# A hybrid encoder layer on one core: the first weight unit in blocks, logits ahead of the last value product, a raw buffer for the last output unit, one GpSimd split at the router's end

## The reference

```python
def token_mixer(x, ...):
    proj = rms_norm(x, norm_g) @ w_in        # dq, dk, dv, nq, nk, nv (512 columns each), gates (2048)
    # differential attention: 4 heads, two softmax maps each, T5 bias
    o = (softmax(q1 k1 + bias) - lam * softmax(q2 k2 + bias)) @ dv
    # lam = exp(sum(lq1*lk1)) - exp(sum(lq2*lk2)) + lambda_init
    y_diff = rms_norm(o, diff_subln) * (1.0 - lambda_init)
    # neighbourhood attention: 8 heads, windows of 8 rows x 16 columns on a grid 64 wide
    y_na = neighborhood_attention(nq, nk, nv, na_rpb)
    merged = g_diff * (y_diff @ w_br_diff) + g_na * (y_na @ w_br_na)
    return x + merged @ w_out

def expert_choice_ffn(h, w_router, w_gate, w_up, w_down):   # h = rms_norm(x, norm2_g)
    aff = softmax(t @ w_router)              # 16 experts
    gate, idx = top_k(aff.T, cap)            # 32 prompt and 64 sample tokens for each expert
    he = silu(xe @ wg) * (xe @ wu)           # EXPERT_FF 2816
    y = zeros.at[idx].add((he @ wd) * gate)
```

## Time and profile before

| | |
|---|---|
| time, median of 3 runs | 2210.21 us (2209.09 to 2210.94) |
| the profiled execution | 2212.8 us, of which its span is 2211.0 us |
| instructions | 27257 |
| mean granted clock of TensorE | 0.987 |
| TensorE busy | 2128.8 us (96%) |
| VectorE busy | 1582.0 us (72%) |
| ScalarE busy | 1370.8 us (62%) |
| GpSimd busy | 238.7 us (11%) |
| chain that ended last | PE 82%, DMA 7%, DVE 6%, ACT 4%, issue 1% |
| data moved | 623.97 MB, mean 282 GB/s |

### The profile page before, as it was taken

One profiled execution on the slowest core, in us unless ns is written; L12 is line 12 of the kernel. 1 busy time (PEld: TensorE's weight loads), 2 busy tenths in 40 slices (PEclk: granted clock), 3 DMA queues, 4 the chain that ended last, 5 costly groups with the idle time before them and its releaser, 6 DMA issues.

```text
span 2211.0 us, 27257 instructions
## 1 busy us (share of the span) xinstructions
PE 2128.8 (96%) x10388; PEld 1592.4 (72%) x10388; DVE 1582.0 (72%) x1249; ACT 1370.8 (62%) x1102; POOL 238.7 (11%) x137
## 2 busy tenths in 40 slices
PE   6999999999968999999999999999999999999997
PEld 5867888887756767777677776767767677777765
DVE  5374363233456888888888888888888888888885
ACT  5364364122225777777777777777777777777764
POOL 2202120000130001010101102011010201101010
PEclk9999999999988999999999999999999999999999
DMA  5111141113436999999999999999999999999995
GB/s 232 58 36 67 58 144 60 64 58 115 162 118 236 373 370 366 376 371 385 364 368 385 367 378 370 373 373 370 378 365 380 365 374 385 367 376 374 375 372 184
DMA packets 71389, 623.97 MB, mean 282 GB/s; under 512 B 8272, under 2 KB 8656, under 8 KB 18608
## 3 DMA queue, kind: packets, MB, share of 16 engines
q1 hardware_dynamic: 63264, 595.62, 69.6%
q0 software_dynamic: 7648, 27.40, 4.4%
q10 hardware_dynamic: 432, 0.34, 0.0%
HBM read 609.70 MB, written 13.63 MB: 282 GB/s over the span
## 4 chain that ended last, share of the span: by engine, by line
PE 82%; DMA 7%; DVE 6%; ACT 4%; issue 1%; POOL 0%; ACTq 0%; SPq 0%; DVEq 0%; POOLq 0%
PE PS L527 25%; PE PS L529 25%; PE PS L528 25%; DMA x_w_raw<-in_w_expert_gate 5%; DVE x_w_low L1160 4%; ACT x_w_high L1090 3%; PE PS L625 2%; PE PS L610 2%; PE PS L872 1%; DMA x_w_raw<-in_w_expert_up 1%; PE PS L638 1%; PE PS L536 1%; PE PS L815 1%; PE PS L736 0%; DMA cst<-in_consts 0%
## 5 line engine op out<-in xcount | busy, mean ns | idle before, releaser
L1160 DVE TENSOR_TENSOR x_w_low<-x_w_raw,x_w_high 128x2048 fp32r<-128x2048 f32 (+1 forms) x382 | 1174.5, 3086 | 241.9 <-ACT x_w_high L1090 239.6
L1090 ACT ACTIVATE x_w_high<-x_w_raw 128x3072 fp32r<-128x3072 f32 (+1 forms) x384 | 980.0, 2558 | 266.2 <-PE PS L529 190.9
L527 PE MATMUL PS<-x_w_high,xT_high 128*96 128x512 f32 (+1 forms) x1536 | 580.5, 378 | 9.7 <-DVE x_w_low L1160 7.6
L529 PE MATMUL PS<-x_w_high,xT_low 128*96 128x512 f32 (+1 forms) x1536 | 575.4, 375 | 0.0
L528 PE MATMUL PS<-x_w_low,xT_high 128*96 128x512 f32 (+1 forms) x1536 | 573.4, 373 | 0.0
L527 PEld LDWEIGHTS PS<-x_w_high,xT_high 128*96 128x96 f32 x1536 | 248.3, 162 | 105.6 <-DVE x_w_low L1160 18.6
L529 PEld LDWEIGHTS PS<-x_w_high,xT_low 128*96 128x96 f32 x1536 | 248.1, 162 | 90.0
L528 PEld LDWEIGHTS PS<-x_w_low,xT_high 128*96 128x96 f32 x1536 | 248.8, 162 | 85.1 <-issue 0.2
L527 PE MATMUL PS<-x_w_high,hidden_high 128*96 128x512 f32 x704 | 281.3, 400 | 0.0
L529 PE MATMUL PS<-x_w_high,hidden_low 128*96 128x512 f32 x704 | 276.7, 393 | 0.0
L528 PE MATMUL PS<-x_w_low,hidden_high 128*96 128x512 f32 x704 | 275.9, 392 | 0.0
(11 more groups left out here) (185 smaller groups left out, 1774.4 us busy)
## 6 DMA issues: line engine op xcount, KB each, us to landing
x_w_raw<-in_w_expert_gate SPq DMA_DIRECT2D x96, 1536.0 KB, 8.4
x_w_raw<-in_w_expert_up SPq DMA_DIRECT2D x96, 1536.0 KB, 8.8
x_w_raw<-in_w_expert_down SPq DMA_DIRECT2D x96, 1536.0 KB, 8.3
x_w_raw<-in_w_expert_gate SPq DMA_DIRECT2D x32, 1024.0 KB, 7.5
x_w_raw<-in_w_expert_up SPq DMA_DIRECT2D x32, 1024.0 KB, 7.4
x_w_raw<-in_w_expert_down SPq DMA_DIRECT2D x32, 1024.0 KB, 7.0
w_raw<-in_w_in SPq DMA_DIRECT2D x20, 1024.0 KB, 4.8
x<-in_x_sample SPq DMA_DIRECT2D x8, 512.0 KB, 13.5
```

The lines of the kernel that those rows point to most:

```text
L527: mm(out, sh, mh, start=first, stop=False)
L529: return mm(out, sl, mh, start=False, stop=last)
L1090: a_(xh[:, w % SPLITS, 0:n], xraw[:, w % RAWS, 0:n], ACT.Copy).then_inc(x_high, 1)
L1160: return v.tensor_tensor(out, src, high.bitcast(F32), ALU.subtract)
```

## The change

1. *Start.* Unit 0 and the first four token blocks are loaded block by block, in turn; the vectors come first on SyncE's queue. ScalarE and VectorE split them block by block, and TensorE works on unit 0 with the block as the outer loop and the six tiles inside. Constants and lambdas move to GpSimd's queue, behind the fourth token block; the bias tables behind the eighth. The clearing of the keys goes to the projection "pn", the lambda steps to the ends of the first two chunks of "pd".
2. *Projection.* In "pd" the transposes come three steps behind instead of two (`LAG`). The last value product of both projections is issued in step 2 of `attend`, behind the logits of items 0 and 1, and its scaling on VectorE in step 1. In "pn" two tiles are normalised behind value tile 0, and none behind the last.
3. *Output.* Unit 27 has a raw buffer of its own, `w_last`, in the place of its low half, and its load doesn't wait for a split. The reload of x is issued two chunks earlier.
4. *Router end.* GpSimd splits unit 0 alone. VectorE takes the low halves of the tokens and of unit 1 before the slot tables; TensorE doesn't wait for the tables before the first expert.

```diff
+LAG = {"pd": 3, "pn": 2}
...
+        w_last = at("w_raw_last", 50112, UNIT).rearrange("p (k n) -> p k n", k=4)
...
             def load_unit(n, src):
+                if n == UNITS - 1:
+                    stage_done(sp, 5)
+                    sp.dma_start(w_last, src.rearrange("p (k c) -> p k c", k=4)).then_inc(S("o", "last_unit_loaded"), 16)
+                    return
+                if n >= 2:
+                    sp.wait_ge(w_split, n - 1)
                 sp.dma_start(wraw[:, n % 2], src.rearrange("p (k c) -> p k c", k=4)).then_inc(w_loaded[n % 2], 16)
 
-            for u in range(2):
-                for i in (2 * u, 2 * u + 1):
-                    sp.dma_start(xT[:, 2 * i:2 * i + 2, :], x_turned[:, 2 * i:2 * i + 2, :]).then_inc(s_xT[i], 16)
-                load_unit(u, src_of("pd", "q", u))
+            sp.dma_start(rows, vectors).then_inc(s_rows, 16)
+            first = src_of("pd", "q", 0).rearrange("p (k c) -> p k c", k=4)
+            for k in range(4):
+                sp.dma_start(xT[:, k, :], x_turned[:, k, :]).then_inc(S("n1", f"xT_loaded{k}"), 16)
+                sp.dma_start(wraw[:, 0, k], first[:, k]).then_inc(S("n1", f"w_loaded{k}"), 16)
+            for i in range(2, 4):
+                sp.dma_start(xT[:, 2 * i:2 * i + 2, :], x_turned[:, 2 * i:2 * i + 2, :]).then_inc(s_xT[i], 16)
+            load_unit(1, src_of("pd", "q", 1))
...
-                if kind == "out0":
+                if kind == "gate_n1":
...
-            sp.wait_ge(w_high, UNITS)
+            sp.wait_ge(w_high, UNITS - 1)
...
+            pool.wait_ge(S("n1", "tev"), 4)
+            pool.dma_start(cst, consts).then_inc(s_cst, 16)
+            pool.dma_start(lamv, lambdas).then_inc(s_lamv, 16)
+            pool.wait_ge(S("n1", "tev"), KD)
             load_diff(0)
             load_diff(1)
-            pool.wait_ge(s_cst, 32)
+            pool.wait_ge(s_cst, 16)
...
-            for w in range(2):
-                n = unit_width(w)
-                pool.wait_ge(x_high, w + 1)
...
+            n = unit_width(0)
+            pool.wait_ge(x_high, 1)
+            nc.gpsimd.tensor_tensor(xl[:, 0, 0:n], xraw[:, 0, 0:n], xh[:, 0, 0:n].bitcast(F32), ALU.subtract
+                                    ).then_inc(x_split, 1)
...
+                if before is None:
+
+                    for k in range(4):
+                        pe.wait_ge(S("n1", "tev"), k + 1)
+                        pe.wait_ge(S("n1", "w_low"), k + 1)
+                        for t in range(NT):
+                            i = split_product(PS[:, t, :], hTh[:, k, t * P:(t + 1) * P], hTl[:, k, t * P:(t + 1) * P],
+                                              wh[:, 0, k], wl[:, 0, k], k == 0, False)
+                            if k == 3:
+                                i.then_inc(w_prod, 1)
+                    pe.wait_ge(s_cst, 16)
...
-                    if before is None or n >= START_EARLY:
+                    if (NT if before is None else START_EARLY) <= n < len(steps) - 1:
                         chunk_product(chunks, c, u, t, hTh, hTl, bank_free)
                     if u == 1 and c < 2:
                         done_at.append(n)
-                    while jt < len(done_at) and n >= done_at[jt] + 2:
+                    while jt < len(done_at) and n >= done_at[jt] + LAG[stage]:
...
                 for step in range(len(L) + 5):
+                    if step == 2:
+                        chunk_product([c for c in CHUNKS if c[0] == stage], 2, 1, NT - 1, hTh, hTl, None)
...
-            pe.wait_ge(S("rt", "tables"), 2)
...
             for k in range(KD):
-                act.wait_ge(s_xT[k // 2], 16)
+                act.wait_ge(*((S("n1", f"xT_loaded{k}"), 16) if k < 4 else (s_xT[k // 2], 16)))
                 a_(hTh[:, k, :], xT[:, k, :], ACT.Copy, scale=g1[:, k:k + 1]).then_inc(S("n1", "high"), 1)
-                if k % 4 == 3:
-                    split_units(k // 4 + 1)
+                if k < 4:
+                    act.wait_ge(S("n1", f"w_loaded{k}"), 16)
+                    a_(wh[:, 0, k], wraw[:, 0, k], ACT.Copy).then_inc(S("n1", "w_high"), 1)
...
+            def keep_values(stage, t):
+                tile = V_ORDER[stage][t]
+                product_done(dve, [c for c in CHUNKS if c[:2] == (stage, "v")][0], t)
+                v.tensor_scalar(vv[:, tile, :], PS[:, t, :], nrs[:, tile:tile + 1], None, ALU.mult
+                                ).then_inc(S(stage, "pused"), 1)
...
+                            if t < NT - 1:
+                                keep_values(stage, t)
+                            for y in {0: (0, 1), 5: ()}.get(t, (t + 1,)) if stage == "pn" else ():
+                                norm_y(y)
                     if c < 2:
                         scale_proj(stage, NT * c + NT - 1)
+                        if stage == "pd":
+                            (lambda_sums, lambda_factor)[c]()
+                        else:
+                            v.memset(kT[c][64 * (1 - c):64 * (2 - c)], 0.0).then_inc(s_kz, 1)
...
+                    if step == 1:
+                        keep_values({"diff": "pd", "na": "pn"}[br], NT - 1)
...
-            dve.wait_ge(S("rt", "slots"), 1)
-            link(table(0, CS, 3, 1, E))
-            v.tensor_scalar(idxs, idxf[0:CS, :], float(SP_), None, ALU.subtract)
-            v.tensor_copy(idxi[:, 2:E + 1], idxf[:, 2:E + 1]).then_inc(S("rt", "tables"), 1)
...
             for q in range(PRE):
                 misc_low("tokens", q, q + 1, q + 1, 6 + q)
-            dve.wait_ge(x_split, RAWS + 2)
+            dve.wait_ge(x_split, RAWS + 1)
+            unit_low(0, 1)
+            dve.wait_ge(S("rt", "slots"), 1)
+            link(table(0, CS, 3, 1, E))
+            v.tensor_scalar(idxs, idxf[0:CS, :], float(SP_), None, ALU.subtract)
+            v.tensor_copy(idxi[:, 2:E + 1], idxf[:, 2:E + 1]).then_inc(S("rt", "tables"), 1)
             unit_low(0, 2)
```

84 lines of the change are left out of this document (42 added, 42 removed).

## The result

The changed kernel took 2197.4 us (median of 4 runs, 2196.1 to 2197.7), the kernel before beside it 2210.6 us (2209.1 to 2211.1): a ratio of 0.9943, 95% interval 0.9929 to 0.9957. That is a gain of 13.2 us where 20.6 were forecast; it moved the way that the prediction said, and ended 0.9 us above the upper end of the range. The profiled execution took 2197.56 us with a span of 2195.8 us, so the span shrank by 15.2 us.

A forecast was written before the change was run, and what follows sets the result against it. TensorE, busy 96% of the span, was taken to bound the kernel. Gains of 8.8, 0.9, 1.4, 4.1 and 5.35 us summed to 20.6, taking the median from 2210.2 to 2189.6 us; range 2184.0 to 2196.5.

The forecast's parts named there:

- What bounds the kernel: Whole kernel: TensorE is busy 96% of the span; the expert loop has no idle time left, so gains come before it.
- Rivals 2 and 4: Expert loop: head start of its loads was needed, 2194, chance 0.10; or its period grows, 2234 at 350 GB/s, chance 0.03.
- Rival 5: Edits don't do what they say, as the same waits end last for another reason: within 0.2%, chance 0.03.
- Start: Before the first matmul: loading and splitting by blocks starts TensorE at 8.4 instead of 17.2 us, 8.8 us gained.
- Rival 1: Kernel start gives 3 to 5 us less, through slow queue filling, stalls between blocks or the identity table; 2193.5, chance 0.15.
- First attention: Where the first attention begins: value product behind logits 0 and 1 gains 0.9 us, bounds 0 and 3.5.
- Rival 3: First attention and router keep the clock up, and the value windows land in time: 5 us more, 2184.5, chance 0.13.
- Second attention: Where the second attention begins: later value product and earlier normalising gain 1.4 us, bounds 0.2 and 2.6.
- 1.85 - 1.6 + 1.2: Second attention: transposes 1.85 us earlier, a new 1.6 us wait for value windows, a 1.2 us bias-table wait gone.
- Output buffer: Output projection: own raw buffer for the last unit removes a 2.7 us wait and 1.4 us of low clock, 4.1 us.
- Router: Router end: a faster comparison gains 3.0 us, low halves of tokens before the tables 1.75 us.
- Clock at the first expert: Start of the expert loop: without the pause the clock may rise earlier, 0 to 2.4 us, taken as 0.6.

## Why the prediction was right or wrong

**What bounds the kernel: right.** The loop kept its length (1533.85 and 1533.1 us), and all but 0.75 us of the gains and losses lie ahead of it. Rivals 2 and 4, which had the loop or its first loads pay for the start, fall: no wait is left at the first experts. Rival 5 falls too.

**Start: 8.8 forecast, 8.44 at the first matmul, 7.4 in the end.** Two things were missed. The rate: from 4 to 8 us the DMA engines moved 236 GB/s with loads of one block, where the kernel before moved 424 in the same time. The summary of that window after, with SyncE's queue (packets, MB, share of the 16 engines), and then that queue before:

```profile
DMA packets 421, 0.94 MB, mean 236 GB/s; under 512 B 47, under 2 KB 47, under 8 KB 421
q1 hardware_dynamic: 421, 0.94, 91.8%
```

```profile
q1 hardware_dynamic: 194, 1.04, 62.4%
```

Part of the gap is that 0.65 of the 1.69 MB came on the other engines' queues before, whose loads are now moved; SyncE's own queue brings hardly less, but in more than twice as many packets, which fill 92% of the engines' time instead of 62%. I had reckoned with 369 to 410 throughout. The first block needs little, so TensorE started only 0.4 us late, but what follows in the queue, unit 2's load last, comes later, and the bias loads (issued at 19.23 us) now share the engines with it. I had given unit 2's split 2.7 us of room through the later transposes; it was used up, and TensorE waited 0.80 us there (0 to 1.01 us in the other kernels with this start). The run with the bias loads moved has q ready at least 2.1 us earlier, which shows that those loads were part of the delay. Against the run with the old start, whose first matmul came at 17.36 us, 1.1 us are lost between the first matmul and the scores: 0.80 are this wait, 0.2 one slow matmul more at the beginning (seven beside six), 0.1 stays open. Rival 1 (3 to 5 us less) named the right mechanism at three times the size.

I had read the Trainium skill (SBUF — State Buffer, the "DVE blocks DMA" trap) as speaking against moving the constants to GpSimd's queue. It names VectorE operations in a 2-port mode, and whether the two-input passes here are of that kind no run shows. The issue at 13.88 us landed 5.4 us later, between VectorE's passes of 1 us, and TensorE waited for nothing there. No run here shows the trap.

**First attention: 0.9 forecast, 0.7 measured by undoing it.** The reading that logits 2 and not the transposes are in the way was right. The trace showed 1.9 us more, which the clock gave; it had been 0.58 and 0.73 in the kernel before from 129 to 139 us, and in the changed kernel it was 1.00 in one execution and 0.66 for 5 us in another, and with windows by rows it was 0.59 and 0.73 again. Rival 3 took this for a gain that the change might bring. It is not the change's: the kernel before with other loads has it too. In the forecast this row stood at nothing, so its 1.9 us are luck of the executions compared.

**Second attention: 1.4 forecast, -4.8 measured.** This is the step that failed. The sum was 1.85 - 1.6 + 1.2. Its first term was even better, 2.44 us (the transposes of s_na came 84.48 us after those of q before, and 82.04 after). The direction of the second was right, its size wrong. TensorE comes 12.52 us earlier than before (312.92 against 300.40, ready) and the windows' first issue 9.44 us earlier (282.69 and 273.25), so TensorE gains 3.1 us on them; I had said 2.85. But I had the last windows landed at 28.6 us after the first issue, worked out from one microsecond of the queue at 0.10 MB near the end. They took 32.4 us. Of these 3.8 us two bias tables are about 2, by the run that held them back. In the kernel before the first of the two was issued 27.0 us after the first windows, when they were nearly through:

```profile
309.65 0.53 POOL L410 DMA_DIRECT2D bias_windows<-in_bias_sample  x1 [12.11 <-DVE small L1283]
```

Now it is issued at 296.96, 23.7 us after them, with 8.7 us to go, and the next at 301.16, with 4.5 to go. The other 1.7 us are not explained by a run; the 28.6 was an estimate, and all that the trace of the kernel before shows is that the windows had landed by 312.92 us, 30.2 us after their first issue. The collision was in my own text: that this load is issued earlier was counted as a gain of 1.2 us, and I didn't ask what it would meet. The third loss wasn't in the sum at all: behind a wait of 5.25 us the clock fell, 3.15 us more (1.7 to 2.9 us in four other traces of this order behind a wait of 5.0 to 5.1 us). Together 1.4 + 0.6 - 3.65 (the wait of 5.25 in place of 1.6) - 3.15 = -4.8. I had priced the clock in three other places and left it out for the wait that I myself had introduced. I had left it out for the old wait of 3.4 us too, since the profiled execution of the kernel before kept its clock there; three other executions with the old order lost some 1.6 us behind it. The root is the form of the window loads: with one row each, and the same new order, the stretch is 3.9 us shorter than before instead of 4.8 longer.

**Output buffer: 4.1 forecast, 4.35 in the traces, 2.9 by undoing it** plus 1.4 of clock that an execution may or may not lose. **Router: 3.0 and 1.75 forecast, 2.94 and 1.84 measured**, each confirmed by its own run (3.0 and 1.85). The rule of the Trainium skill (SBUF — State Buffer, SBUF: two separate sides, on the shared pair) that I had weighed there agrees with the trace: 3673 ns for the comparison with GpSimd's second split beside it, 680 ns without. **Clock at the first expert: 0.6 forecast, 0.75** left over between the spans.

**The median.** In spans I was off by 5.4 us, of which the second attention is 6.2 and the start 1.4, against small gains elsewhere and 1.9 us of clock. The rest of the miss, 2.4 us, is the step from the span to the median: I carried over that the profiled execution lay 2.6 us above the median, while the one of the changed kernel lay 0.15 us above its own. It was an execution with 1.92 + 1.42 us of low clock that others don't have, but it also kept the clock behind the 3.4 us wait; which of this put it above the median isn't shown. 2189.6 + 5.4 + 2.4 = 2197.4. Without this step the forecast's errors would have given 2195.0 us, inside the range; the 1.9 us of clock were good luck on the other side.

**Slips in the working.** The share of the DMA engines in the loop is 0.98 in the earlier trace rows, not 0.97. Rival 3's terms add up to 5.75 us more, not 5, which is 2183.9 us and below the range. Neither touches the forecast.
